# The four weight buffers of a two-model forward pass, each set 64 bytes further from the one before it

## The reference

```python
for i in range(4):
    x = x + rms_norm(mixer_i(rms_norm(x, g[i, 0])), g[i, 1])      # h @ w_in, recurrence, o @ w_out
    h = rms_norm(x, g[i, 2])
    x = x + rms_norm(square(relu(h @ mlp_w1[i])) @ mlp_w2[i], g[i, 3])
for l in range(2):
    x = x + swiglu(...)     # silu(h @ w_gate) * (h @ w_up), then @ w_down
    x = x + hybrid_mixer(...)
    x = x + cross_attention(..., mem)
    x = x + swiglu(...)
```

## Time and profile before

| | |
|---|---|
| median of 3 runs | 2706.51 us |
| the runs | 2715.36, 2706.51, 2691.03 us |
| span of the profiled execution | 2705.3 us |
| TensorE, matmul row | 2625.5 us busy, 97%, 21582 instructions |
| TensorE, weight loads | 2553.7 us, 94%, 21582 |
| VectorE | 1660.7 us, 61%, 1970 |
| ScalarE | 1351.4 us, 50%, 1663 |
| GpSimd | 152.2 us, 6%, 224 |
| HBM read | 441.21 MB, 166 GB/s with what is written |

### The profile page before, as it was taken

The page is one execution under the profiler, slowest core; times in us unless marked ns, Lnnn a source line. Parts: engine busy times, 40 slices in busy tenths (PEclk is TensorE's granted clock), DMA queues, the critical chain, the costliest instruction groups (busy, mean ns, idle before and its releaser), DMA issues.

```text
span 2705.3 us, 48788 instructions
## 1 busy us (share of the span) xinstructions
PE 2625.5 (97%) x21582; PEld 2553.7 (94%) x21582; DVE 1660.7 (61%) x1970; ACT 1351.4 (50%) x1663; POOL 152.2 (6%) x224
## 2 busy tenths in 40 slices
PE   8989999999998999989999999999999999999998
PEld 8979999899997999988999999989999999999998
DVE  5657655475575754676755665766665657764664
ACT  5645545454436544663544444554545446544543
POOL 4400000000000000330000000000000000000000
PEclk9999999999999999999999999999999999999999
DMA  7514564456643565442565756434766655334663
GB/s 214 162 33 141 187 234 133 152 176 211 211 144 121 179 219 186 144 147 94 171 216 178 191 187 211 152 125 141 196 194 187 189 199 159 126 130 142 188 188 125
DMA packets 429970, 451.96 MB, mean 167 GB/s; under 512 B 13346, under 2 KB 395024, under 8 KB 427584
## 3 DMA queue, kind: packets, MB, share of 16 engines
q1 hardware_dynamic: 417952, 416.12, 49.2%
q0 software_dynamic: 7312, 32.35, 3.5%
q10 hardware_dynamic: 4496, 0.39, 0.1%
HBM read 441.21 MB, written 7.60 MB: 166 GB/s over the span
## 4 chain that ended last, share of the span: by engine, by line
PE 85%; DVE 6%; ACT 4%; POOL 2%; DMA 1%; issue 1%; ACTq 0%; SPq 0%; DVEq 0%
PE ps L593 85%; ACT wH L1440 2%; DVE wL L2064 2%; POOL arena L497 1%; ACT hidden_parts L1500 1%; PE ps L1037 0%; POOL arena L499 0%; DMA ring<-in_gdn_w_in 0%; DVE arena L2484 0%; DMA arena<-tiles_out 0%; DVE arena L2592 0%; DMA arena<-leaf_out 0%; DMA leaf_out<-arena 0%; POOL arena L507 0%; DVE arena L2335 0%
## 5 line engine op out<-in xcount | busy, mean ns | idle before, releaser
L2064 DVE TENSOR_TENSOR wL<-ring,wH 128x2048 fp32r<-128x2048 f32 x392 | 898.4, 2292 | 781.2 <-ACT wH L1440 780.8
L1440 ACT ACTIVATE wH<-ring 128x2048 fp32r<-128x2048 f32 x392 | 752.4, 1919 | 1050.6 <-PE ps L593 1048.6
L593 PE MATMUL ps<-hidden_parts,wH 128*128 128x256 f32 x6656 | 1005.0, 279 | 4.1 <-ACT hidden_parts L1500 2.7
L593 PEld LDWEIGHTS ps<-hidden_parts,wH 128*128 128x128 f32 x6656 | 910.8, 188 | 6.1 <-issue 3.6
L593 PE MATMUL ps<-hidden_parts,wL 128*128 128x256 f32 x3328 | 700.4, 279 | 1.0 <-DVE wL L2064 1.0
L593 PEld LDWEIGHTS ps<-hidden_parts,wL 128*128 128x128 f32 x3328 | 525.4, 188 | 1.4 <-DVE wL L2064 1.4
L593 PE MATMUL ps<-hH,wH 128*128 128x256 f32 x2624 | 369.5, 282 | 7.1 <-DVE hH L2081 5.0
L593 PE MATMUL ps<-hH,wL 128*128 128x256 f32 x2624 | 361.6, 279 | 2.2 <-DVE wL L2064 2.2
L593 PEld LDWEIGHTS ps<-hH,wH 128*128 128x128 f32 x2624 | 331.4, 189 | 16.6 <-issue 15.9
L593 PE MATMUL ps<-hL,wH 128*128 128x256 f32 x2624 | 347.0, 278 | 0.0
L593 PEld LDWEIGHTS ps<-hH,wL 128*128 128x128 f32 x2624 | 329.2, 189 | 2.9 <-DVE wL L2064 2.8
(11 more groups left out here) (301 smaller groups left out, 1965.2 us busy)
## 6 DMA issues: line engine op xcount, KB each, us to landing
ring<-in_mlp_w SPq DMA_DIRECT2D x128, 1024.0 KB, 5.4
ring<-in_ffn_w_gate SPq DMA_DIRECT2D x88, 512.0 KB, 3.9
ring<-in_ffn_w_up SPq DMA_DIRECT2D x88, 512.0 KB, 5.2
ring<-in_ffn_w_down SPq DMA_DIRECT2D x44, 1024.0 KB, 5.0
ring<-in_gdn_w_in SPq DMA_DIRECT2D x32, 1024.0 KB, 5.9
ring<-in_w_in SPq DMA_DIRECT2D x28, 1024.0 KB, 5.4
hidden_parts<-mem_parts POOLq DMA_DIRECT2D x14, 1024.0 KB, 7.5
ring<-in_mlstm_w_in SPq DMA_DIRECT2D x12, 1024.0 KB, 5.2
```

What stands on the lines that cost most here:

```text
L593: return pe.matmul(o, l, r, start=start, stop=stop, **k)
L1440: f(wH[:, n % PARTS, :], ring[:, n % RING, :], ACT.Copy).then_inc(sem("high_split"), 1)
L2064: tt(wL[:, n % PARTS, :], ring[:, n % RING, :], wH[:, n % PARTS, :].bitcast(F32), ALU.subtract)\
```

## The change

The four slots become slices of one tensor, `weights`, in the order high of slot 0, low of slot 0, high of slot 1, low of slot 1, with 16 floats (64 bytes) of gap between one and the next. `headR`, 8 floats, moves from behind the masks into the first gap. Everything behind the weights starts 192 bytes higher, `cumR` 160. The instructions of every engine, their order, their shapes and their waits are the same ones, and so are the DMAs; the names `wH`, `wL` and `headR` are `weights` afterwards. The diff of the names in the places that use them is left out but for one.

```diff
+STEP = 16
...
-        wH = sb("wH", [P, PARTS, SLAB], F32R)
-        wL = sb("wL", [P, PARTS, SLAB], F32R)
+        weights = sb("weights", [P, 2 * PARTS * (SLAB + STEP) - STEP], F32R)
...
-        headR = sb("headR", [P, 8], F32R)
+        headR = weights[:, SLAB:SLAB + 8]
...
+        def half_of(n, low):
+            at = (2 * (n % PARTS) + low) * (SLAB + STEP)
+            return weights[:, at:at + SLAB]
...
-                return wH[:, n % PARTS, :].rearrange("p (c n) -> p c n", c=c)
+                return half_of(n, 0).rearrange("p (c n) -> p c n", c=c)
```

More of the change, by code:

```diff
@@ L596, in high @@
                 pe.wait_ge(sem("high_split"), n + 1)
-                return wH[:, n % PARTS, :].rearrange("p (c n) -> p c n", c=c)
+                return half_of(n, 0).rearrange("p (c n) -> p c n", c=c)
             def low(n, c):
-                return wL[:, n % PARTS, :].rearrange("p (c n) -> p c n", c=c)
+                return half_of(n, 1).rearrange("p (c n) -> p c n", c=c)
             def three(dst, w, x, chunks, before=None, first=True, last=True, second="x"):
@@ L1296, in slab_piece @@
                             pe.wait_ge(sem("low_split"), n + 1)
-                        w = (wL if turn == 2 else wH)[:, n % PARTS, :].rearrange("p (c n) -> p c n", c=DC)
+                        w = half_of(n, int(turn == 2)).rearrange("p (c n) -> p c n", c=DC)
                         x = hL if turn == 1 else hH
@@ L1439, in split @@
                         act.wait_ge(sem("products_done"), slabs[n - PARTS][5])
-                    f(wH[:, n % PARTS, :], ring[:, n % RING, :], ACT.Copy).then_inc(sem("high_split"), 1)
+                    f(half_of(n, 0), ring[:, n % RING, :], ACT.Copy).then_inc(sem("high_split"), 1)
                 split_upto[0] = max(split_upto[0], upto)
@@ L2063, in split @@
                     dve.wait_ge(sem("high_split"), n + 1)
-                    tt(wL[:, n % PARTS, :], ring[:, n % RING, :], wH[:, n % PARTS, :].bitcast(F32), ALU.subtract)\
+                    tt(half_of(n, 1), ring[:, n % RING, :], half_of(n, 0).bitcast(F32), ALU.subtract)\
                         .then_inc(sem("low_split"), 1)
```

## The result

The changed kernel takes **2740.64 us** (median of four runs, 2735.18 to 2740.70); the kernel before took 2706.98 us in the same comparison. The ratio is **1.0145, interval 1.0105 to 1.0185**: slower by 34 us. That is 39 us above the predicted 2702, on the side of the rival "the conflict repeats every 128 bytes" (2744), and inside the range, which had been drawn out to hold that rival.

What follows compares the result with a forecast made beforehand. TensorE's pace through its 18,816 pairs of weight load and matmul was taken to bound the kernel. The terms, 15.9 - 20.1 = -4.2 us, set against the median of 2706.5, gave 2702 us, range 2666 to 2750.

Steps and rivals of the forecast that it cites:

- the conflict repeats every 128 bytes: Rival for TensorE's pairs: distances 128 and 256 act like 0, 9664 pairs at +4.7 ns, put at 2744 us; chance 0.29.
- What bounds the kernel: TensorE's pace through 18,816 pairs of weight load and matmul sets the time; its matmul row is busy 2625.5 of 2705.3 us.
- The address as the cause: The byte distance between a pair's moving stream and next weight load in SBUF sets and picks TensorE's pace, 113.1 to 120.0 ns.
- Part 1: 3392 pairs, mostly `hidden_parts` with odd high weights, come to distance 0: 120.0 ns against 115.3, +15.9 us.
- Part 2: 9152 pairs come to distances 128, 192 and 256, which the trace never shows, and take 113.1 ns: -20.1 us.
- Part 3: 6272 pairs stay at distance 64 and 115.3 ns: 0, or -13.8 inheriting 113.1, or +13.8 all at 117.5.
- Part 4: Everything else, such as fp32 passes, cumR matmuls and the weight splits of DVE and ACT hidden behind PE: costed at 0.
- a repeat at 256 bytes: Aside to the 128-byte rival: 4832 pairs at 120 (+22.7) and 7712 at 113 (-17.0) would give 2712 us.
- No conflict left: Faster rival: the 9152 pairs at middle distances fall to 109.2 ns, -56 us, giving 2666 us; chance 0.20.
- No effect: Rival: the fillers' 120 ns is their own and paces depend on how the stream starts, 2706 us; chance 0.09.
- my own case: Distance 0 slow, distances further apart at 113.1 ns: 2702 us, its own range 2680 to 2728; chance 0.42.
- What would show it: Down products at 120 ns in odd slabs, 113 in even ones, alternating every 5.5 us; 113 in products with hH and hL.

Runs made afterwards that it cites:

- u0_all_at_0: The kernel before with all four weight buffers 64 bytes lower, so that every pair reads its operands at distance 0; 2777.57 us, ratio 1.0268.
- uniform kernels: The kernel before with buffers moved so that every pair has one distance, 0, 128, 192 or 256 bytes: 2777.57, 2757.23, 2726.37 and 2782.87 us.
- TensorE by itself: Small kernel without the main computation: TensorE alone runs sections of 192 pairs at distances from 0 to 512 bytes; 113.3 to 123.3 ns per pair.
- hid64_activations_moved: The kernel before with `hidden_parts` and the arena 64 bytes higher and the weights unmoved, so pairs with `hidden_parts` come to distance 0; 2749.05 us, ratio 1.0153.
- second small kernel: TensorE alone again, varying what stands between sections and putting single pairs of another distance into a stream at 64; that stream ran at 113.3 or 117.8 ns.
- stagger_alone: The kernel before with only the four weight buffers set 64 bytes apart, `hidden_parts` and arena where they were; 2739.64 us, ratio 1.0125.
- arena192_alone: The kernel before with only everything behind the weights 192 bytes higher, so pairs with `hidden_parts` come to distance -128; 2729.43 us, ratio 1.0092.
- small kernels: Two kernels without the main computation, TensorE alone running pairs at chosen distances with float32 matmuls between sections; 113.3 or 117.8 ns per pair at distance 64.

## Why the prediction was wrong

**What bounds the kernel: right.** The pace of the pairs is the time: 36.6 of the 39.7 us that PE gained are in it, and `u0_all_at_0`, with each pair 4.4 ns longer, is 74 us longer.

**The address as the cause: right.** The uniform kernels and TensorE by itself show it. The Trainium skill ("SBUF — State Buffer", section "SBUF: two separate sides") has contention between engines at the port pair of DVE and GpSimd alone, and PE never waiting on anyone. No run here shows PE held up by another engine at SBUF, but its own two reads have a price by address that the section does not name: moving the activations' buffer by 64 bytes cost 42 us in `hid64_activations_moved`. The Trainium skill ("TensorE: Matmul & The Clock Gate", Part 2) has the next load take nothing from the running matmul; the trace does not agree, with 113.3 to 123.3 ns for one shape by the distance of the two. Its formula gives 109.2 ns for 256 columns as an estimate, but it is stated there for an isolated matmul, not for a stream of pairs; the lowest steady pace of these pairs in any run here was 113.3.

**Part 1, distance 0, +15.9 us: right in kind, 5 us too large.** The price of a pure stream is 120.0 as read from the filler rows; measured in place were 118.8 ns and +11 us, in the down products because these pairs stand in threes with one at 64, and the cycle (0, 0, 64) runs at 117.8 ns even by itself. So the objection in the rival, that a single pair at distance 0 costs nothing visible, was a hint that prices do not add up pair by pair.

**Part 2, distances 128, 192 and 256, -20.1 us: this step failed.** I took 113.1 ns, "if distance 0 is always slow and 64 sometimes, further apart should be the good case". It measured 115.7 to 118.8 ns, +14 us, an error of 34 us, most of the 39 that the forecast missed. Two things were wrong in it. I had no row for these distances, only the ends 120.0 and 109.2, and picked a value from a picture of nearness that nothing in the trace bore out; and that picture was false, since 256 is distance 0 again (119.97 ns uniform) and 128 a poor place of its own (118.7). One row could have warned me and I gave it to the rival: +64 and -64 have the same two paces. A relation that wraps round would do that, though one that is alike on both sides of zero would too; and of 64-byte steps with a wrap at 256 bytes only 64 and 192 are not 0 or 128.

**Part 3, distance ±64 unchanged, 0: failed to the other end.** It measured +11 us against a bound of +13.8. I had named the inheritance, but from pairs at 113.1. The pairs ahead turned out to be at 0 and 128, and one pair at 0 sends the stream to 117.8, as the second small kernel shows. In the changed kernel 30% of the `hH` and `hL` pairs at 64 run at 113.3, where it was 61%. Its trace bears the reason out in place: blocks of pairs at 64 that follow directly on a block at 256, which is distance 0 again, run at 117.7 ns in the mean (42 blocks, and 86 in `stagger_alone` at the same 117.7), those behind a block at 128 at 116.5 (67; 116.9 in `stagger_alone`). At 192 it is the other way round: 114.0 ns behind 256, 117.7 behind 128. So what a pair costs depends on the pairs ahead of it, and no price per distance can hold for all.

**Part 4, everything else, 0: right.** Splits at 2292 and 1916 ns, waits of PE for DVE's weights 4.3 us.

**The rivals.** "Repeats every 128 bytes" named the time (2744) and its mechanism halfway: 0 and 256 are one case, 128 is nearly as bad, but the period is 256 and the prices are below 120 in a mixed stream. I counted 9664 pairs at +4.7 ns for it; the loss is spread thinner over more pairs. My aside, that a repeat at 256 bytes would give 2712, had the period right and failed at the same term, since it put 128 and 192 at 113 ns. "No conflict left" fell: no pair got below 113.3. "No effect" fell as well. That my range held the result is the rival's doing: my own case ended at 2728.

**What would show it:** the alternation every 5.5 us is there, but at 115.6 and 117.9 instead of 113 and 120, and 113 in the products of `hH` and `hL` is not.

**What stays open.** Why the pace follows the distance of TensorE's two operands modulo 256 bytes; why one distance has two paces; what in a stretch of float32 matmuls turns one into the other, why two pairs at 128 undo what one does, and why eight of eight pushes did nothing in one SwiGLU. In `hid64_activations_moved` the pairs at 64 got better behind pairs at 0 (84% at 113.3). A float32 stretch between would turn 117.8 into 113.3, which fits, but `arena192_alone`, with -128 bytes in the place of 0, has the same 84%, and I have no reason for both.

## What to carry to other kernels

Where TensorE is busy for over 95% of the span, count matmuls in equal windows: two counts for one shape at one granted clock are a pace to be won, and a mean over the run hides it. A distance (or a size, or a period) that the trace never shows has no good default; its cost lies between the bounds, and if the relation wraps round, the new places may be the bad one again, so run the kernel with all accesses at one distance before mixing several. Here the layout was already at the best distance of those tried, and what was left to gain came from steering which of its two paces it fell into.

## What the runs showed of the hardware that I had not expected

- A stream of fp32r pairs, a weight load of 128x128 and a matmul of 128x256, runs at 113.3 to 123.3 ns per pair with TensorE alone at work and the clock granted at 1.00, by the byte distance of the two operands modulo 256. 0 is 120.0 and 48 was 123.3 in one kernel, 117.8 in another; none was steadily below 113.3.
- Distance 64 has two steady paces, 113.3 and 117.8 ns. A stretch of one to eight float32 matmuls turned one into the other in 63 of 64 places of the small kernels; one pair at distance 0 set 117.8; one at 128 set 113.3 there, and in five of seven places of the whole kernel.
- A mixed stream has a price of its own: the cycle (-128, -128, -64) runs at 115.6 ns, where streams of 128 alone take 120.0 or 118.6 and of 192 alone 117.8. In the changed kernel blocks at 192 run at 114.0 ns behind 256 and at 117.7 behind 128.
- The whole kernel is 74 to 79 us (2.7 to 2.9%) longer when a few hundred bytes of padding at most are moved so that all operands lie at distance 0 or 256, and 20 us shorter with 16 superfluous matmuls than without them.
